# The indexer's projections cut into column blocks of 256 and 328 instead of 512 and 72

## The chip, the cores and the metric

The kernel runs on one core of one Trainium2 chip. The metric is the device time of one execution in microseconds (us). The core's engines are named as the profile names them: PE multiplies matrices (PEld is its weight load), DVE is the vector engine, ACT the activation engine, POOL the general one, SP issues DMAs. Work is ordered between engines by semaphores that the program sets by hand.

## The reference

One transformer block with a sparse attention, a gated unit and experts is followed by two more layers of another kind. The change touches the beginning of the first block alone, the projections of the attention's indexer, with 256 tokens of width 1024:

```python
proj = xn @ w_in[l]
q, k, v, qi, ki, wi, su, sv, ga, gb = split_columns(proj)
qi = rope(qi.reshape(B, L, IDX_HEADS, IDX_DIM), positions)   # 8 heads of 64
ki = rope(ki[:, :, None, :], positions)[:, :, 0]             # one head of 64
...
rel = jax.nn.relu(jnp.einsum('bqhd,bsd->bqhs', qib, ki))
score = jnp.einsum('bqh,bqhs->bqs', wb, rel).astype(jnp.float32)
_, sel = lax.top_k(score, top_k)
```

`qi` has 512 columns, `ki` 64 and `wi` (the gate of each indexer head) 8; they stand side by side in `w_in`. The score of each earlier token chooses the 64 keys that the attention sees.

## The kernel before

**Blocks and units.** `weight_block` cuts the weights into column blocks of up to 512 columns (L127), in the order in which they are used: q0, q1, qi, kw, k0, k1, v0, v1 and so on. A block of 1024 rows is one piece of the ring: SP loads it into one of two raw slots. It is then split into four units of two row chunks each. For each unit ACT rounds the raw numbers to the matmul's input type (`w_high`, L1517), POOL subtracts to get the rest (`w_low`, L852), and PE multiplies: per row chunk k and token tile t three matmuls, high times high (L925), high times w_low (L926) and x_low times w_high (L927). A block of eight chunks is 48 matmuls, whatever its width; the width is the number of columns that each streams. PE starts a unit when its `w_low` is made; POOL goes through the units in order; SP loads piece n when all `w_low` of piece n - 2 are made (`raw_free`). The product of a block lies in one of two pairs of PSUM banks, by the parity of the block's number, and the next block of the same parity waits until it has been moved out (`lin_moved`).

**What stands between the blocks.** DVE first works out the rotation angles (L2068 to L2082), in which each of the two token tiles begins with a multiplication of the frequencies by the position, from SBUF to SBUF (L2072). ACT takes sine and cosine of them (L1612, L1613), then copies q1 out of PSUM (L1539), then makes the w_high of kw (L1517), then takes its share of the transposes of the gated unit's weights `sgu_w` (L1615). Those are four jobs of two 128x128 transposes each on PE (L973), called by `sgu_weights` within qi at its chunks 4 and 5, two jobs at each; DVE copies the first and the third out of PSUM (L2091) and ACT the second and the fourth. There are two PSUM buffers for such jobs, so the third waits until DVE has taken the first, the fourth until ACT has taken the second. POOL masks the transposed weights after the fourth (L859), and its queue has this mask between the w_low of qi and those of kw.

**The rotation.** When qi is done DVE rotates its eight heads with `rotate_block` (L2101, L2102, L2104: two multiplications and one sum for each half of a head and each token tile, 12 instructions), then frees the bank, which k0 waits for. When kw is done DVE makes `wi` (L2112) and rotates the one key head, writing it twice side by side into `ki_twice`. k0 transposes both at its chunk 6, after later constants: `turn("qi", 4, ...)` and `turn("ki", 1, ...)`. After k1, PE forms the scores of the eight indexer heads (L1094).

Of the kernel before, what the change touches and what calls it, by code (L numbers as in the profile page):

```python
# [25 lines left out]
ALU = mybir.AluOpType  # L26
# [3 lines left out]
P = 128  # L30
SEQ = 256
TILES = SEQ // P
# [88 lines left out]
def program(nc, io, upto=99, tap=None):  # L121
# [3 lines left out]
    def weight_block(name, sources, width):  # L125


        rows = sources[0][0].shape[0]
        used = []
        for k0 in range(0, rows // P, 8):  # L130
            kn = min(8, rows // P - k0)
            loads, at = [], 0
            for w, c0, n in sources:
                loads.append((kn, width, at, n, w[k0 * P:(k0 + kn) * P, c0:c0 + n].rearrange("(k p) n -> p k n", p=P)))
                at += n
            used.append((len(pieces), k0, kn))
            pieces.append(loads)
        blocks[name] = (len(blocks), used, width)
# [2 lines left out]
    starts = dict(q=0, k=1024, v=2048, qi=3072, kw=3584, su=3656, sv=4680, ga=5704, gb=6728)  # L141
    for name in ("q", "k", "v", "su", "sv", "ga", "gb"):
        if name == "k":
            weight_block("qi", [(w_in, starts["qi"], 512)], 512)
            weight_block("kw", [(w_in, starts["kw"], 72)], 72)
        for j in range(2):
            weight_block(f"{name}{j}", [(w_in, starts[name] + j * NB, NB)], NB)

# [88 lines left out]
    with ctx:  # L237
# [70 lines left out]
        def buf(i, words=2048, at=0):  # L308
            return work[:, 2048 * i + at:2048 * i + at + words]

        def tok(view, t=TILES):
            return view.rearrange("p (t n) -> p t n", t=t)
# [131 lines left out]
        scaled_x = tok(buf(5))  # L444
        merged = tok(buf(4))
        v_tok, su, sv, ga, gb = (tok(buf(i)) for i in (5, 6, 7, 8, 9))
        qi_roped = tok(buf(9, 1024, 1024))
        qi_T = feat(buf(8, 1024))
        ki_twice = tok(buf(8, 256, 1168))
        ki_T = buf(8, 512, 1424).rearrange("p (e s) -> p e s", e=2)  # L450
        y_attn = tok(buf(2))
        relu2 = attn[:, 0:1024].rearrange("p (b t s) -> p b t s", b=2, t=TILES)
# [150 lines left out]
        def lin_out(name):  # L603
            o, _, width = blocks[name]
            return lin_ps[:, 2 * (o % 2):2 * (o % 2) + 2, 0:width]
# [297 lines left out]
        def _(pe):  # L903
            def linear(name, high, low, ready=None, rows_apart=0):


                o, used, width = blocks[name]
                if o >= 2:
                    pe.wait_ge(lin_moved[o % 2], o // 2)
                out = lin_out(name)  # L910
                last_k = used[-1][1] + used[-1][2] - 1
                block_units = [(k0 + UNIT_K * i, unit) for n, k0, _ in used for i, unit in enumerate(unit_views(n))]

                def products(first_k, unit, rows, prepare):
                    u, slot, words, _ = unit
                    if prepare:
                        pe.wait_ge(low_made, u + 1)
                    wh, wl = (w[:, slot, 0:words].rearrange("p (k n) -> p k n", n=width) for w in (w_high, w_low))
                    for j in range(words // width):
                        k = first_k + j  # L920
                        if ready and prepare:
                            ready(k)
                        for t in rows:
                            at = slice(P * t, P * (t + 1))
                            pe.matmul(out[:, t, :], high(k)[:, at], wh[:, j, :], start=(k == 0), stop=False)  # L925
                            pe.matmul(out[:, t, :], high(k)[:, at], wl[:, j, :], start=False, stop=False)  # L926
                            mm = pe.matmul(out[:, t, :], low(k)[:, at], wh[:, j, :], start=False, stop=(k == last_k))  # L927
                    return mm

                together = len(block_units) - rows_apart  # L930
                for first_k, unit in block_units[:together]:
                    products(first_k, unit, range(TILES), True).then_inc(units_used, 1)
                if rows_apart:
                    for first_k, unit in block_units[together:]:
                        mm = products(first_k, unit, (0,), True)
                    mm.then_inc(first_rows, 1)
                    for first_k, unit in block_units[together:]:
                        products(first_k, unit, (1,), False).then_inc(units_used, 1)
# [26 lines left out]
            def turn(name, n, src, first=0):  # L965

                for i in range(first, n):
                    k = jobs[name] + i
                    if k >= 2:
                        pe.wait_ge(tr_moved[k % 2], k // 2)  # L970
                    for c0, view in src(i):
                        rows_in_view = view.shape[0]
                        mm = pe.transpose(tr_ps[0:view.shape[1], k % 2, c0:c0 + rows_in_view], view,  # L973
                                          ident[0:rows_in_view, 0:rows_in_view])
                    mm.then_inc(tr_done, 1)
# [10 lines left out]
            def made(name):  # L986
                return lambda k: parts_made(pe, name, k + 1)

            def both(x):

                return lambda i: [(P * t, x[:, t, P * i:P * (i + 1)]) for t in range(TILES)]

            def small_out(pe, name):

# [58 lines left out]
            def amid(at, *what):  # L1053

                def ready(k):
                    if k == at:
                        for do in what:
                            do()
                return ready
# [22 lines left out]
            def later_columns():  # L1082
                pe.wait_ge(later_rows_in, 16 * (len(row_loads()) - 1))
                turn("later_cols", 1, lambda i: [(0, rows[0:104, 0, :]), (104, rows[0:120, 1, :]), (224, rows[0:88, 2, :])])

            linear("k0", *from_x, ready=amid(6, later_columns, lambda: pe.wait_ge(roped, 2), lambda: turn("qi", 4, both(qi_roped)),
                                             lambda: turn("ki", 1, both(ki_twice))))
            linear("k1", *from_x)
            tr_wait(pe, "ki", 1)
            for i in range(IDX_HEADS):  # L1090
# [878 lines left out]
        def _(dve):  # L1969
            order = [0]  # L1970

            def step(ins):

                order[0] += 1
                ins.then_inc(dve_order, 1)
                dve.wait_ge(dve_order, order[0])
# [116 lines left out]
            def rotate_block(dst, src, heads, cos, sin):  # L2093

                m = sc_ps[:, 0, 0:32 * heads].rearrange("p (h j) -> p h j", h=heads)
                for t in range(TILES):
                    x = src[:, t, :].rearrange("p (h a j) -> p h a j", h=heads, a=2)
                    c, s = (cs[:, t, :].unsqueeze(1).broadcast_to([P, heads, 32]) for cs in (cos, sin))
                    for a, op in ((0, ALU.subtract), (1, ALU.add)):
# [3 lines left out]
                        for y in (*others, first):  # L2103
                            step(dve.tensor_tensor(y, first, m, op))  # L2104

            lin_ready(dve, "qi")
            rotate_block(lambda t: [qi_roped[:, t, :].rearrange("p (h a j) -> p h a j", h=IDX_HEADS, a=2)], lin_out("qi"),
                         IDX_HEADS, cos1[:, :, 64:96], sin1[:, :, 64:96])
            dve.sem_inc(lin_moved[blocks["qi"][0] % 2], 1)
            dve.sem_inc(roped, 1)  # L2110
            lin_ready(dve, "kw")
            step(dve.tensor_tensor(wi[:], lin_out("kw")[:, :, 64:72], rest.unsqueeze(2).broadcast_to([P, TILES, IDX_HEADS]), ALU.mult))  # L2112
            rotate_block(lambda t: [ki_twice[:, t, 64 * c:64 * c + 64].rearrange("p (h a j) -> p h a j", h=1, a=2)
                                    for c in range(2)], lin_out("kw")[:, :, 0:64], 1, cos1[:, :, 64:96], sin1[:, :, 64:96])
            dve.sem_inc(lin_moved[blocks["kw"][0] % 2], 1)
            dve.sem_inc(roped, 1)
            step(dve.memset(ki_T, 0.0))
            dve.wait_ge(tr_done, jobs["later_cols"] + 1)
            dve.tensor_copy(cols[:, KC:312], tr_ps[:, jobs["later_cols"] % 2, KC:312]).then_inc(tr_moved[jobs["later_cols"] % 2], 1)
# [527 lines left out]
```

## Time and profile before

| | us |
| --- | --- |
| median of 3 runs | 1339.53 |
| lowest and highest run | 1337.6 and 1340.6 |
| span of the profiled execution | 1341.4 |
| PE busy in it | 1252.6 (93%) |
| POOL busy | 770.9 (57%) |
| ACT busy | 639.0 (48%) |
| DVE busy | 461.8 (34%) |

The span runs from the first to the last instruction of one profiled execution; it lies 1.9 us above the median of the timed runs and 0.8 us above the slowest of them. PE is the busiest engine by far, but its busy time counts a matmul from its start to its modelled end, so that matmuls overlap in it: how fast PE goes is read from the distance between the starts of two. The granted clock of PE (PEclk) is a share of 2.4 GHz; the profile shows two levels, 1.00 and 0.50 (1.2 GHz).

### The profile page before, as it was taken

The numbers are of one execution on the slowest core, as the hardware profiler recorded it, in microseconds if no ns is written. First come the engines' busy times: TensorE is split into PE (matmuls) and PEld (weight loads), VectorE is DVE, ScalarE is ACT, GpSimd is POOL, SyncE is SP. The second block draws the span as 40 slices with busy tenths as digits, with TensorE's granted clock in tenths as the row PEclk, the third lists the DMA queues.
The fourth block names the chain that finished last, engine by engine and source line by source line (L and its number), as shares of the span: only waits on it lengthen the run. The fifth ranks groups of instructions, "written<-read, shape, count | busy, mean of one in ns | idle before, by whom it ended". The sixth has DMA issues, their size and how long they took to land.

```text
span 1341.4 us, 19669 instructions
## 1 busy us (share of the span) xinstructions
PE 1252.6 (93%) x7904; PEld 1029.7 (77%) x7904; DVE 461.8 (34%) x1047; ACT 639.0 (48%) x1108; POOL 770.9 (57%) x345
## 2 busy tenths in 40 slices
PE   8999999998887887999899999999999889999998
PEld 6888877776342333887789999888997778999986
DVE  3527333433121112355613332102468272322311
ACT  6445544643111011745636655436797444655552
POOL 5868985440000000982048988888689805788884
PEclk8999999998998999998999999999999999999999
DMA  6635554396999999553034655644535503455552
GB/s 241 218 128 189 188 189 158 110 367 262 423 421 420 414 422 412 184 182 111 1 106 147 227 183 178 219 162 153 183 129 186 187 19 124 142 179 185 189 188 79
DMA packets 126449, 275.09 MB, mean 205 GB/s; under 512 B 7524, under 2 KB 53916, under 8 KB 114076
## 3 DMA queue, kind: packets, MB, share of 16 engines
q1 hardware_dynamic: 126076, 272.86, 55.8%
q8 instruction: 58, 0.95, 0.3%
q10 hardware_dynamic: 288, 1.05, 0.2%
q14 instruction: 27, 0.22, 0.0%
HBM read 272.85 MB, written 1.05 MB: 204 GB/s over the span
## 4 chain that ended last, share of the span: by engine, by line
PE 75%; ACT 7%; DMA 7%; DVE 5%; POOL 4%; issue 2%; POOLq 0%; SPq 0%; DVEq 0%; ACTq 0%
PE lin_ps L925 11%; PE lin_ps L927 11%; PE lin_ps L926 11%; PE lin_ps L955 8%; PE lin_ps L958 8%; PE lin_ps L957 8%; DMA ring<-in_w_expert_in 5%; PE sc_ps L1218 4%; POOL w_low L852 4%; ACT w_high L1517 2%; PE lin_ps L1235 2%; PE lin_ps L1041 2%; PE sc_ps L1010 2%; PE lin_ps L1203 1%; PE tr_ps L1020 1%
## 5 line engine op out<-in xcount | busy, mean ns | idle before, releaser
L852 POOL TENSOR_TENSOR w_low<-ring,w_high 128x1024 fp32r<-128x1024 f32 (+1 forms) x318 | 762.1, 2432 | 551.5 <-ACT w_high L1517 551.3
L1517 ACT ACTIVATE w_high<-ring 128x1024 fp32r<-128x1024 f32 (+1 forms) x320 | 312.8, 1043 | 139.0 <-PE lin_ps L927 78.7
L955 PE MATMUL lin_ps<-x_high,w_high 128*128 128x256 f32 x960 | 272.8, 284 | 0.0
L957 PE MATMUL lin_ps<-x_high,w_low 128*128 128x256 f32 x960 | 271.6, 283 | 0.0
L958 PE MATMUL lin_ps<-x_low,w_high 128*128 128x256 f32 x736 | 208.3, 283 | 0.0
L957 PEld LDWEIGHTS lin_ps<-x_high,w_low 128*128 128x128 f32 x960 | 184.2, 192 | 0.1
L955 PEld LDWEIGHTS lin_ps<-x_high,w_high 128*128 128x128 f32 x960 | 184.2, 192 | 0.1
L925 PE MATMUL lin_ps<-w_high,x_high 128*128 128x512 f32 (+1 forms) x432 | 170.5, 395 | 5.6 <-POOL w_low L852 2.7
L926 PE MATMUL lin_ps<-w_low,x_high 128*128 128x512 f32 (+1 forms) x432 | 168.1, 389 | 0.0
L927 PE MATMUL lin_ps<-w_high,x_low 128*128 128x512 f32 (+1 forms) x368 | 143.1, 389 | 0.0
L958 PEld LDWEIGHTS lin_ps<-x_low,w_high 128*128 128x128 f32 x736 | 141.2, 192 | 0.0
L925 PEld LDWEIGHTS lin_ps<-w_high,x_high 128*128 128x128 f32 x432 | 82.0, 190 | 22.9 <-DVE w_low L2059 2.8
L926 PEld LDWEIGHTS lin_ps<-w_low,x_high 128*128 128x128 f32 x432 | 82.2, 190 | 15.9
L927 PEld LDWEIGHTS lin_ps<-w_high,x_low 128*128 128x128 f32 x368 | 70.1, 191 | 14.4
L1218 PE MATMUL sc_ps<-ring,work 128*32 128x512 f32 x496 | 62.6, 642 | 14.6 <-DMA ring<-in_w_expert_in 10.2
L1798 ACT ACTIVATE attn<-lin_ps,cols 128x256 f32<-128x256 f32 x44 | 18.5, 472 | 114.7 <-PE lin_ps L958 114.7
L925 PE MATMUL lin_ps<-w_high,hidden_high 128*128 128x512 f32 x176 | 68.7, 390 | 0.7 <-POOL w_low L852 0.7
L926 PE MATMUL lin_ps<-w_low,hidden_high 128*128 128x512 f32 x176 | 68.5, 389 | 0.0
L927 PE MATMUL lin_ps<-w_high,hidden_low 128*128 128x512 f32 x176 | 68.5, 389 | 0.0
L2413 DVE SCALAR_TENSOR_TENSOR attn<-lin_ps,cols,attn 128x255 f32<-128x255 f32 x44 | 21.1, 479 | 124.9 <-ACT attn L1798 124.9
L958 PE MATMUL lin_ps<-u_low,w_high 128*128 128x256 f32 x224 | 63.4, 283 | 0.0
L1218 PEld LDWEIGHTS sc_ps<-ring,work 128*32 128x32 f32 x496 | 16.5, 117 | 53.2 <-issue 38.8
(430 smaller groups left out, 1921.7 us busy)
## 6 DMA issues: line engine op xcount, KB each, us to landing
ring<-in_w_expert_in SPq DMA_DIRECT2D x31, 2048.0 KB, 14.3
ring<-in_ffn_w_in SPq DMA_DIRECT2D x44, 1024.0 KB, 7.7
ring<-in_w_in SPq DMA_DIRECT2D x13, 2048.0 KB, 7.8
ring<-in_b_w_in SPq DMA_DIRECT2D x11, 2048.0 KB, 8.0
work<-in_w_expert_out SPq DMA_DIRECT2D x8, 2048.0 KB, 23.0
ring<-in_w_expert_out SPq DMA_DIRECT2D x8, 2048.0 KB, 17.6
ring<-in_ffn_w_out SPq DMA_DIRECT2D x8, 2048.0 KB, 8.0
ring<-in_a_w_in SPq DMA_DIRECT2D x4, 2048.0 KB, 8.2
```

The lines of the kernel that those rows point to most:

```text
L852: pool.tensor_tensor(w_low[:, slot, 0:words], raw, w_high[:, slot, 0:words].bitcast(F32), ALU.subtract).then_inc(low_made, 1)
L925: pe.matmul(out[:, t, :], high(k)[:, at], wh[:, j, :], start=(k == 0), stop=False)
L926: pe.matmul(out[:, t, :], high(k)[:, at], wl[:, j, :], start=False, stop=False)
L927: mm = pe.matmul(out[:, t, :], low(k)[:, at], wh[:, j, :], start=False, stop=(k == last_k))
L955: pe.matmul(out, wh[:, j, at], high(k), start=(k == 0 and f < 2), stop=False, skip_group_check=True)
L957: pe.matmul(out, wl[:, j, at], high(k), start=False, stop=False, skip_group_check=True)
L958: mm = pe.matmul(out, wh[:, j, at], low(k), start=False, stop=(k == last_k), skip_group_check=True)
L1010: mm = pe.matmul(sc_ps[:, g % 2, SEQ * t:SEQ * t + n], q(i, t), k(i)[:, 0:n], start=True, stop=True)
L1041: mm = pe.matmul(out[:, dim * t:dim * (t + 1)], pT[:, P * n:P * (n + 1)], v(i, c), start=(c == 0), stop=(c == chunks[-1][0]))
L1218: mm = pe.matmul(hid_ps[CAP * e:CAP * (e + 1), :], gathered[:, 4 * a + k, CAP * e:CAP * (e + 1)], extra_slot(e)[:, k, :] if extra and a == ...
L1235: mm = pe.matmul(y_ps[CAP * e:CAP * (e + 1), n, :], act_T[:, P * f + CAP * e:P * f + CAP * (e + 1)], w, start=(f == 0), stop=(f == 1))
L1517: act.activation(w_high[:, slot, 0:words], raw, ACT.Copy).then_inc(high_made, 1)
```

## The change

The same 584 columns are projected in two blocks of another cut. qi now has the first 256 columns (four query heads); kw has the other 328 (four query heads, the key, the gate). Both are still 48 matmuls and four units. `rotate_block` runs on four heads after qi, and on five (four query heads and the key) after kw, and one more DVE copy doubles the rotated key. The rotated heads of kw lie in a new view `qk_roped`, which replaces `ki_twice`; the transposes read from both views, as many as before.

```diff
-            weight_block("qi", [(w_in, starts["qi"], 512)], 512)
-            weight_block("kw", [(w_in, starts["kw"], 72)], 72)
+            weight_block("qi", [(w_in, starts["qi"], 256)], 256)
+            weight_block("kw", [(w_in, starts["qi"] + 256, 328)], 328)
...
-        qi_roped = tok(buf(9, 1024, 1024))
+        qi_roped = tok(buf(9, 512, 1024))
+        qk_roped = tok(buf(6, 768, 1024))
         qi_T = feat(buf(8, 1024))
-        ki_twice = tok(buf(8, 256, 1168))
...
-            linear("k0", *from_x, ready=amid(6, later_columns, lambda: pe.wait_ge(roped, 2), lambda: turn("qi", 4, both(qi_roped)),
-                                             lambda: turn("ki", 1, both(ki_twice))))
+            linear("k0", *from_x, ready=amid(6, later_columns, lambda: pe.wait_ge(roped, 2), lambda: turn("qi", 2, both(qi_roped)),
+                                             lambda: turn("qi", 4, both(qk_roped, 2), first=2),
+                                             lambda: turn("ki", 1, both(qk_roped, -2))))
...
             lin_ready(dve, "kw")
-            step(dve.tensor_tensor(wi[:], lin_out("kw")[:, :, 64:72], rest.unsqueeze(2).broadcast_to([P, TILES, IDX_HEADS]), ALU.mult))
...
+            step(dve.tensor_tensor(wi[:], lin_out("kw")[:, :, 320:328], rest.unsqueeze(2).broadcast_to([P, TILES, IDX_HEADS]), ALU.mult))
+            rotate_block(lambda t: [qk_roped[:, t, 0:320].rearrange("p (h a j) -> p h a j", h=5, a=2)],
+                         lin_out("kw")[:, :, 0:320], 5, cos1[:, :, 64:96], sin1[:, :, 64:96])
             dve.sem_inc(lin_moved[blocks["kw"][0] % 2], 1)
-            dve.sem_inc(roped, 1)
+            dve.tensor_copy(qk_roped[:, :, 320:384], qk_roped[:, :, 256:320]).then_inc(roped, 1)
             step(dve.memset(ki_T, 0.0))
```

The order of the queues stays; the sizes in them change. On POOL, from the first constants to the block v1 (`w_low` is the rest of a unit's weights, `xqT` holds the gated unit's transposed weights):

```order
 L840 MEMSET eps 128x1
-L852 TENSOR_TENSOR w_low<-ring,w_high 128x1024 x10
+L852 TENSOR_TENSOR w_low<-ring,w_high 128x1024 x6
+L852 TENSOR_TENSOR w_low<-ring,w_high 128x512 x4
 L859 AFFINE_SELECT xqT<-xqT 128x1024
-L852 TENSOR_TENSOR w_low<-ring,w_high 128x144 x4
+L852 TENSOR_TENSOR w_low<-ring,w_high 128x656 x4
 L852 TENSOR_TENSOR w_low<-ring,w_high 128x1024 x16
```

The four units of qi halve and the four of kw grow from 144 to 656 columns; the mask still stands between them.

On ACT, from the sine to the first units behind kw, before:

```order
L1612 ACTIVATE attn<-sc_ps 128x192
L1613 ACTIVATE attn<-sc_ps 128x192
L1539 ACTIVATE work<-lin_ps,small 128x512 x2
L1517 ACTIVATE w_high<-ring 128x144 x4
L1615 ACTIVATE xqT<-tr_ps 128x256 x2
```

and after (every line number of ACT is one higher):

```order
L1613 ACTIVATE attn<-sc_ps 128x192
L1614 ACTIVATE attn<-sc_ps 128x192
L1540 ACTIVATE work<-lin_ps,small 128x512 x2
L1518 ACTIVATE w_high<-ring 128x656 x4
L1616 ACTIVATE xqT<-tr_ps 128x256 x2
```

The two copies of transposed weights (`xqT`) stay behind the w_high of kw, which are 656 columns wide now.

## Rows read from the trace of the kernel before

**Rows 1.** The page's part 4: the chain that ended last, by engine.

```profile
PE 75%; ACT 7%; DMA 7%; DVE 5%; POOL 4%; issue 2%; POOLq 0%; SPq 0%; DVEq 0%; ACTq 0%
```

**Rows 2.** Timeline of PE, qi to k0: start us, us, engine, line, instruction, [idle before].

```profile
37.32 0.39 PE L925 MATMUL lin_ps<-w_high,x_high 128*128 128x512 f32 x1
...
42.76 0.60 PE L973 MATMUL tr_ps<-ident,work 128*128 128x128 f32 x4
...
44.59 0.60 PE L973 MATMUL tr_ps<-ident,work 128*128 128x128 f32 x4
...
49.27 0.28 PE L927 MATMUL lin_ps<-w_high,x_low 128*128 128x72 f32 x1
...
54.30 0.28 PE L927 MATMUL lin_ps<-w_high,x_low 128*128 128x72 f32 x1
54.95 0.72 PE L925 MATMUL lin_ps<-w_high,x_high 128*128 128x512 f32 x1 [0.36 <-DVEq L2109]
...
58.70 0.39 PE L925 MATMUL lin_ps<-w_high,x_high 128*128 128x512 f32 x1
...
64.83 0.66 PE L973 MATMUL tr_ps<-ident,work 104*128 104x104 f32 x5
...
70.11 0.39 PE L925 MATMUL lin_ps<-w_high,x_high 128*128 128x512 f32 x1
```

**Rows 3.** Stretch of k0: length; busy PE, PEld, DVE, ACT, POOL; PEclk; DMA share; GB/s.

```profile
54.95:58.46 3.51, 3.51 (x9) 2.73 (x10) 2.83 (x15) 0.43 (x1) 3.51 (x3) 0.51 0.26 96
```

**Rows 4.** Timeline of PE in the second feed-forward: matmuls of 256 columns.

```profile
759.77 0.28 PE L955 MATMUL lin_ps<-x_high,w_high 128*128 128x256 f32 x1
...
761.93 0.28 PE L955 MATMUL lin_ps<-x_high,w_high 128*128 128x256 f32 x1
```

**Rows 5.** Timeline of DVE: the end of the angles, their scaling, the two rotations.

```profile
34.85 2.25 DVE L2072 TENSOR_SCALAR work<-work,pos_f 128x96 f32<-128x96 f32 x1
...
40.11 0.27 DVE L2082 TENSOR_SCALAR sc_ps<-sc_ps 128x96 f32<-128x96 f32 x1
41.00 1.60 DVE L2090 TENSOR_SCALAR attn<-attn,small 128x32 f32<-128x32 f32 x4 [0.62 <-ACT attn L1613]
...
49.34 0.42 DVE L2101 TENSOR_TENSOR work<-lin_ps,attn 128x256 f32<-128x256 f32 x1 [3.90 <-PE lin_ps L927]
...
56.26 0.19 DVE L2101 TENSOR_TENSOR work<-lin_ps,attn 128x32 f32<-128x32 f32 x1
```

**Rows 6.** Timeline of POOL: units of qi, the mask, units of kw, of k0 and k1.

```profile
32.26 9.47 POOL L852 TENSOR_TENSOR w_low<-ring,w_high 128x1024 fp32r<-128x1024 f32 x4 [0.79 <-ACT w_high L1517]
45.68 1.09 POOL L859 TENSOR_SCALAR_AFFINE_SELECT xqT<-xqT 128x1024 f32<-128x1024 f32 x1 [3.95 <-ACT xqT L1615]
46.75 1.86 POOL L852 TENSOR_TENSOR w_low<-ring,w_high 128x144 fp32r<-128x144 f32 x4
50.90 18.78 POOL L852 TENSOR_TENSOR w_low<-ring,w_high 128x1024 fp32r<-128x1024 f32 x8 [2.28 <-ACT w_high L1517]
```

**Rows 7.** Timeline of ACT: units of qi, the sine, q1, units of kw, k0, k1.

```profile
31.12 3.91 ACT L1517 ACTIVATE w_high<-ring 128x1024 fp32r<-128x1024 f32 x4 [1.00 <-DMA ring<-in_w_in]
...
40.41 0.33 ACT L1612 ACTIVATE attn<-sc_ps 128x192 f32<-128x192 f32 x1 [4.08 <-DVE sc_ps L2082]
...
40.85 1.27 ACT L1539 ACTIVATE work<-lin_ps,small 128x512 f32<-128x512 f32 x2
41.99 0.98 ACT L1517 ACTIVATE w_high<-ring 128x144 fp32r<-128x144 f32 x4
...
49.76 3.91 ACT L1517 ACTIVATE w_high<-ring 128x1024 fp32r<-128x1024 f32 x4 [4.15 <-DMA ring<-in_w_in]
58.03 3.91 ACT L1517 ACTIVATE w_high<-ring 128x1024 fp32r<-128x1024 f32 x4 [4.36 <-DMA ring<-in_w_in]
```

**Rows 8.** Timeline of PE late in the program: a wait, after which the clock is low.

```profile
1103.03 0.66 PE L1428 MATMUL tr_ps<-ident,work 128*128 128x128 f32 x2 [2.09 <-DVE o_low L2603]
```

**Rows 9.** Stretch after that wait, columns as in rows 3.

```profile
1103.00:1106.00 3.00, 2.97 (x8) 2.47 (x9) 0.76 (x2) 0.48 (x1) 0.00 (x0) 0.50 0.00 0
```

More of the change, by code:

```diff
@@ L987, in made, with both @@
                 return lambda k: parts_made(pe, name, k + 1)
-            def both(x):
-                return lambda i: [(P * t, x[:, t, P * i:P * (i + 1)]) for t in range(TILES)]
+            def both(x, before=0):
+                return lambda i: [(P * t, x[:, t, P * (i - before):P * (i - before + 1)]) for t in range(TILES)]
             def small_out(pe, name):
@@ L2106, in _ @@
             lin_ready(dve, "qi")
-            rotate_block(lambda t: [qi_roped[:, t, :].rearrange("p (h a j) -> p h a j", h=IDX_HEADS, a=2)], lin_out("qi"),
-                         IDX_HEADS, cos1[:, :, 64:96], sin1[:, :, 64:96])
+            rotate_block(lambda t: [qi_roped[:, t, :].rearrange("p (h a j) -> p h a j", h=4, a=2)], lin_out("qi"),
+                         4, cos1[:, :, 64:96], sin1[:, :, 64:96])
             dve.sem_inc(lin_moved[blocks["qi"][0] % 2], 1)
@@ L2111, in _ @@
             lin_ready(dve, "kw")
-            step(dve.tensor_tensor(wi[:], lin_out("kw")[:, :, 64:72], rest.unsqueeze(2).broadcast_to([P, TILES, IDX_HEADS]), ALU.mult))
-            rotate_block(lambda t: [ki_twice[:, t, 64 * c:64 * c + 64].rearrange("p (h a j) -> p h a j", h=1, a=2)
-                                    for c in range(2)], lin_out("kw")[:, :, 0:64], 1, cos1[:, :, 64:96], sin1[:, :, 64:96])
+            step(dve.tensor_tensor(wi[:], lin_out("kw")[:, :, 320:328], rest.unsqueeze(2).broadcast_to([P, TILES, IDX_HEADS]), ALU.mult))
+            rotate_block(lambda t: [qk_roped[:, t, 0:320].rearrange("p (h a j) -> p h a j", h=5, a=2)],
+                         lin_out("kw")[:, :, 0:320], 5, cos1[:, :, 64:96], sin1[:, :, 64:96])
             dve.sem_inc(lin_moved[blocks["kw"][0] % 2], 1)
-            dve.sem_inc(roped, 1)
+            dve.tensor_copy(qk_roped[:, :, 320:384], qk_roped[:, :, 256:320]).then_inc(roped, 1)
             step(dve.memset(ki_T, 0.0))
```

## The prediction

> **What bounds the kernel now.** I read the chain of work that ended last first: three quarters of it is PE [rows 1]. So a change in the first block's projections is worth what it takes from PE's timeline there, and after it from whatever PE waits for. Then I read PE's timeline from the start of qi to the start of k1 [rows 2]. qi begins at 37.32 and has done 24 of its 48 matmuls at 42.76: 5.44 / 24 = 0.227 us each. kw goes in steps of (54.30 - 49.27) / 45 = 0.112 us, though it streams a seventh of the columns. Then k0 waits 0.36 us for DVE and starts at 54.95, and its first nine matmuls take until 58.70, 0.417 us each. The granted clock says why: in that stretch it is 0.51, the lower of the two levels [rows 3], and what PE did before was kw's 48 narrow matmuls and the short wait. k1 starts at 70.11. Last come the queues that feed the stretch: DVE's angles and rotations [rows 5], POOL's units [rows 6], ACT's [rows 7].
>
> **PE's own work.** A matmul of 256 columns goes at (761.93 - 759.77) / 18 = 0.120 us [rows 4]. No row shows 328 columns. Bounds are 0.120 and 0.227; on the line between them it is 0.120 + 72 / 256 x 0.107 = 0.150, which I take, since the nearer row is 256 (by the lower bound kw would be 1.4 us shorter, by the upper 3.7 longer). qi: 48 x (0.227 - 0.120) = 5.1 saved. kw: 48 x (0.150 - 0.112) = 1.8 paid. Taken alone that is 3.3 us less.
>
> The Trainium skill, TensorE: Matmul & The Clock Gate, section "Back-to-back issue gap", gives N / 2.4 + 2.5 ns for a gap. By it, 256 columns are 109 ns and 328 are 139; the trace's 120 for 256 differs and decides, and by the page's figure kw would be 48 x 11 ns = 0.5 us shorter and the time 1337.5, an estimate from that page.
>
> **A wait takes most of it.** The transposes of sgu_w stand inside qi, at its chunks 4 and 5, and they need other engines that do not come sooner because PE does. PE would reach the first pair at 37.32 + 24 x 0.120 = 40.2 instead of 42.76. It can do jobs 1 and 2, six matmuls and job 3; job 4 needs ACT to have copied job 2, and ACT's queue has sine, cosine, the copy of q1 and the w_high of kw ahead of that copy, the last now 656 columns wide instead of 144. So the end hangs on DVE's angles, which start ACT's sine.
>
> DVE: the second multiplication of L2072 began at 34.85 and took 2.25 us, eight times the 0.27 of a neighbour of the same width [rows 5]. It ended at 37.10, while POOL's second unit of qi ended at 32.26 + 2 x 2.37 = 37.00 [rows 6]: it was held until that unit was over. With 512 columns a unit takes, on the line from 0.465 (144) to 2.37 (1024), 1.26 us. POOL was free from 31.47 (0.79 before 32.26), and ACT, which waited 1.00 for the weights until 31.12 [rows 7], is ready at 30.12 when half the bytes are to land. So the units end at 32.7, 34.0, 35.26 and 36.5, and DVE is let go at 35.36, 1.74 us sooner. The angles end at 38.64 instead of 40.38. The Trainium skill, SBUF — State Buffer, section "SBUF: two separate sides", calls the ports that DVE and GpSimd share an exclusive lock, held for a whole instruction. By that rule the gain is these 1.74 us and the second rival below is out; the trace's 0.10 between the two ends agrees, and that it is one pair of ends keeps the rival in.
>
> ACT: all is 1.74 sooner up to kw, so q1 is copied from 39.11 and the units of kw start at 40.25. One takes, between 0.245 and 0.98 [rows 7], 0.67; four end at 42.94, just as before (41.99 + 0.98). Copying job 2 takes some 0.4: 43.3. PE has by then stood since about 41.4, 1.9 us.
>
> POOL: from the start of the second pair of jobs to the mask it was 45.68 - 44.59 = 1.09; with one job only left, some 0.85. The mask starts at 44.2, the units of kw 1.07 later at 45.3, each 1.57 long (the same line): the first is made at 46.84, the last at 51.6. PE ends qi at 43.3 + 0.3 + 18 x 0.120 = 45.8, waits 1.1 for the first unit, and does kw in 48 x 0.150 = 7.2, until 54.1; POOL's later units are ahead of it. k0 starts at 54.2 instead of 54.95: **0.75 us** sooner. Of 3.3 + 0.5 us, about 3 went into the two waits.
>
> **The clock.** If kw at 328 columns keeps PE at the full level, the nine matmuls of k0 take 9 x 0.227 instead of 3.75: **1.7 us** less. Bounds: 0 (it falls all the same, or the timed runs of before don't pay it) to 1.7. From there to k1 nothing changes in length: 36 matmuls and the 5.28 us from 64.83 to 70.11 [rows 2]. k1 starts at 54.2 + 8.2 + 5.3 = 67.7 instead of 70.1.
>
> **What is late next.** DVE rotates four heads after qi: at 128 columns, between 0.19 and 0.42 [rows 5], about 0.33 a step with its wait, 12 steps, 4.0 us from 46.0: done at 50, so k0 waits for nothing there, where it did before. After kw come wi, 12 steps of 160 columns (0.36), 4.5 us: 58.8. The new copy of the key is SBUF to SBUF, as L2072 is, so it can be held by a unit of POOL for up to 2.37: 61.2. PE asks for it at chunk 6 of k0, 54.2 + 8.2 = 62.4. It costs nothing with 1.2 us in hand, and up to 1 us if kw ends late against POOL. The weights: k0 is loaded once qi's w_low are made, which is sooner; ACT found k0 landed at 49.76 and POOL is not free for it before 51.6. k1 is loaded once kw's w_low are made, 51.6 instead of 48.61 (46.75 + 1.86), so it lands about 3 us later than 58.03 at most, and ACT ends its units at 65 at most, where it should copy the first transposes of k0 at 63: between 0 and 0.7 us on PE through the fourth of those jobs; I take 0.1. Load issues, semaphores and the memory layout I cost at nothing: as many DMAs of as many rows, and SP still has the same small loads ahead of k0.
>
> **Sum.** On the profiled execution 0.75 + 1.7 - 0.1 = 2.35 us, 1341.4 to 1339.05. What follows is fed by PE's own progress, so I carry it whole. The median of before lies 1.9 below this span, and whether the timed runs pay the low clock at k0 no row shows. I count half of it: 0.75 + 0.85 - 0.1 = 1.5, and 1339.5 - 1.5 = **1338.0**.
>
> **The rivals.**
> 1. *It does what it says:* PE is 3.3 shorter in its matmuls, the 0.5 before k0 and the 1.7 of clock go, no wait comes instead: 5.5 us, 1334.0. This needs job 4 and POOL's first unit of kw in time for a PE that is 2.6 us ahead. Against it: ACT's queue. 8%.
> 2. *Slower:* the angles don't come sooner, because DVE is not let in between two of POOL's short units. The units of kw on ACT then end at 44.7, job 2 is copied at 45.1, the first w_low of kw comes at 48.5, and PE stands 3.6 us. After a wait of 2.09 the clock was low elsewhere [rows 8, 9], so the rest of qi at about 0.21 us a matmul ends at 49.2 and part of kw is slow: k0 starts near 57, 2 us late, less the half of the clock that it had lost: 1340.7. It decides at a release of DVE after about 36.2. For it: nothing but a lock that I read from two ends; against it, the same rows. 15%.
> 3. *The clock falls in the new 1.9 us wait* (the nearest rows: [rows 8, 9]): the rest of qi takes 3.8 instead of 2.2, of which 1.1 is hidden by the wait for kw, and some of kw may be slow, together 0.5 to 1.3: 1338.9. 17%.
>
> The other 5% is for what no row here shows.
>
> **How the numbers follow.** The forecast has 55%. The three runs of before spread 1.9 below and 1.1 above the median, and the clock term is 0.85 either way: the forecast reaches from 1336 to 1340. With rival 2 and its spread above, and a third of what rival 1 adds below, 8 in 10 lie in 1335.5 to 1341.2. A measurement can tell 0.2%, 2.7 us, from no change. Faster by that: rival 1 and the lowest quarter of the forecast, 22%. Slower: the upper end of rival 2, 6%. Within: 72%.
>
> **What would show it.** After the change: L2072's second instruction at 0.5 us instead of 2.25; PE idle about 1.9 before a transpose in qi, put down to ACT's copy, and about 1.1 before kw's first matmul, put down to POOL; 328 columns at 0.150; k0 without a wait and at clock 1.00; k1 near 67.7. The forecast is wrong if the waits in qi and kw together are under 1 us or over 4.5, or if k0 is slow all the same.

## The result and the profile after

| | before | after |
| --- | --- | --- |
| median, us | 1340.70 (22 runs) | 1343.47 (22 runs) |
| lowest to highest, us | 1337.6 to 1343.6 | 1338.71 to 1346.44 |
| span of the profiled execution, us | 1341.4 | 1342.3 |

The ratio after to before is 1.0018, with a 95% interval of 1.0010 to 1.0025: the changed kernel is slower, by a fifth of a per cent. 1338.0 was forecast, in a range up to 1341.2. The line numbers of PE, POOL and SP are those of before, those of ACT and DVE one higher; in an experiment they move by the lines that its edit adds.

**PE** first, the timeline that answers to [rows 2] (start us, us, engine, line, instruction, [idle before <- who ended it]):

```profile
36.78 0.28 PE L925 MATMUL lin_ps<-w_high,x_high 128*128 128x256 f32 x1
...
42.66 0.44 PE L973 MATMUL tr_ps<-ident,work 128*128 128x128 f32 x2 [1.47 <-ACT xqT L1616]
...
46.38 0.39 PE L925 MATMUL lin_ps<-w_high,x_high 128*128 128x328 f32 x1 [1.14 <-POOL w_low L852]
46.61 0.31 PE L926 MATMUL lin_ps<-w_low,x_high 128*128 128x328 f32 x1
...
53.50 0.31 PE L927 MATMUL lin_ps<-w_high,x_low 128*128 128x328 f32 x1
57.52 0.77 PE L925 MATMUL lin_ps<-w_high,x_high 128*128 128x512 f32 x1 [3.71 <-POOL w_low L852]
...
68.63 0.66 PE L973 MATMUL tr_ps<-ident,work 104*128 104x104 f32 x5
```

Up to the end of kw it goes as forecast. From qi's start to kw's last matmul are 53.50 - 36.78 = 16.72 us, with one wait in qi and one before kw; before it was 54.30 - 37.32 = 16.98. Then PE stands 3.71 us before k0, where it stood 0.36 [rows 2]. From qi's start to k0's transposes are 68.63 - 36.78 = 31.85 us against 64.83 - 37.32 = 27.51: 4.3 us are lost in this stretch.

The wait is put down to POOL. POOL's timeline answers to [rows 6] (the last unit of q1 and the four of qi, the four of kw, the first three of k0):

```profile
28.53 7.42 POOL L852 TENSOR_TENSOR w_low<-ring,w_high 128x1024 fp32r<-128x1024 f32 x5
...
44.66 6.27 POOL L852 TENSOR_TENSOR w_low<-ring,w_high 128x656 fp32r<-128x656 f32 x4
55.02 7.03 POOL L852 TENSOR_TENSOR w_low<-ring,w_high 128x1024 fp32r<-128x1024 f32 x3 [4.09 <-ACT w_high L1518]
```

POOL waited 4.09 us for ACT. ACT's timeline answers to [rows 7]:

```profile
39.65 2.69 ACT L1518 ACTIVATE w_high<-ring 128x656 fp32r<-128x656 f32 x4
...
53.89 3.90 ACT L1518 ACTIVATE w_high<-ring 128x1024 fp32r<-128x1024 f32 x4 [10.37 <-PE lin_ps L927]
```

ACT stood 10.37 us before k0's units. The name behind that wait is PE, whose kw block ended at about the same time; what ACT also waited for is k0's weights, as the timeline of the DMA queue of SP tells. First of before (kw's load, the first long ones of the small loads, k0's load):

```profile
31.50 0.37 SPq L665 DMA_DIRECT2D ring<-in_w_in  x1
...
32.54 0.87 SPq L676 DMA_DIRECT2D router_w<-in_w_router_expert  x1
33.45 0.86 SPq L701 DMA_DIRECT2D work<-in_norm_g  x1
...
40.89 0.47 SPq L710 DMA_DIRECT2D cs<-in_rope_sin  x1
41.76 0.37 SPq L665 DMA_DIRECT2D ring<-in_w_in  x1
```

The same of after:

```profile
30.97 0.37 SPq L665 DMA_DIRECT2D ring<-in_w_in  x1
...
32.01 1.54 SPq L676 DMA_DIRECT2D router_w<-in_w_router_expert  x1
33.59 2.85 SPq L701 DMA_DIRECT2D work<-in_norm_g  x1
...
43.03 0.47 SPq L710 DMA_DIRECT2D cs<-in_rope_sin  x1
43.54 0.47 SPq L665 DMA_DIRECT2D ring<-in_w_in  x1
```

The issues of kw's and of k0's weights of after by the view of DMA issues (KB, us from issue to landing); in before they were 288 KB in 3.6 us and 2048 KB in 7.9:

```profile
ring<-in_w_in SPq DMA_DIRECT2D x1, 1312.0 KB, 6.2
...
ring<-in_w_in SPq DMA_DIRECT2D x1, 2048.0 KB, 10.2
```

Between the two loads SP issues the same nineteen small ones. Two of them take (1.54 - 0.87) + (2.85 - 0.86) = 2.66 us longer, now that the load ahead of them has 1312 KB instead of 288. In before SP was done with them at 41.36, just before the slot of k0's load came free with qi's last w_low (32.26 + 9.47 = 41.73 [rows 6]). In after that slot is free at 28.53 + 7.42 = 35.95, by POOL's row of qi's units, and SP comes at 43.54: what k0's load waits for is no longer POOL but SP. The load then takes 10.2 us instead of 7.9. It lands at 53.8, when PE has finished kw; ACT's and POOL's first units add the rest of the 3.71 us. So of the 4.1 us by which it lands later, 1.8 are the later issue and 2.3 the load itself.

Where the 2.3 us are, the landings in the trace tell. A load counts as landed when the last of its sixteen parts is in. In after fifteen parts of k0's load were in at 52.12 and the last at 53.78; in before these were 49.63 and 49.65. So 1.6 us are one late part. The DMA queue that the profile names "instruction" moved one packet of 16 KB in that time, from 51.41 and for 1.06 us. This goes together in all sixteen traces: of the 113 loads into the ring that land between 15 and 100 us, 21 have a last part 0.8 us or more behind the fifteenth, and in each of the 21 such a packet had begun while the load was under way. That the packet is what holds the part up is argued from this and not shown. In before the packet fell into k1's load (from 53.82), for which PE did not wait. For the rest of the 2.3 us the trace has only that at 44 to 46 us the DMA engines are still busy with the small loads (share 0.67 at 95 GB/s).

The clock is low behind the wait: it fell within it, between 56 and 57 us. The stretch of k0 that answers to [rows 3] (length; busy PE, PEld, DVE, ACT, POOL; PEclk; DMA share; GB/s):

```profile
57.50:63.60 6.10, 6.08 (x14) 4.84 (x15) 2.56 (x5) 4.18 (x5) 6.10 (x3) 0.50 0.09 35
63.60:68.60 5.00, 5.00 (x23) 4.08 (x22) 0.00 (x0) 0.00 (x0) 5.00 (x3) 1.00 0.62 200
```

Fourteen matmuls of k0 run at the low level, nine before. From k0's start to its transposes are 11.11 us instead of 9.88. So the 4.3 us are: 3.4 more wait before k0, 1.2 more low clock in it, and 0.3 saved up to kw's end.

The spans differ by 0.9 only. A part of the rest is in stretches that have nothing to do with the change: over the whole span the mean granted clock was 0.984 in the profile of before and 0.992 in that of after. At 311 us, for one, it was low in before and not in after (columns as above). Of before:

```profile
311.10:317.80 6.70, 6.70 (x33) 6.70 (x33) 4.31 (x27) 5.22 (x5) 0.00 (x0) 0.50 1.01 429
```

and of after:

```profile
311.10:317.80 6.70, 5.25 (x43) 4.75 (x42) 4.51 (x16) 5.34 (x9) 0.00 (x0) 1.00 0.78 293
```

Why it falls there in one execution and not in another these runs don't say. The medians differ by 2.8; how the 4.3 us of the one trace become that over 22 runs no trace shows.

### The profile page after: what moved, and what is told of

Read it like the earlier page. It is cut to its first block, busy times and chain, and to the rows that moved or that the text cites. A ratio compares the mean times of both kernels' runs of the same rounds, so it can differ in the third digit from the quotient of the medians.

```text
span 1342.3 us, 19665 instructions
## 1 busy us (share of the span) xinstructions
PE 1244.6 (93%) x7904; PEld 1023.1 (76%) x7904; DVE 459.8 (34%) x1044; ACT 637.4 (47%) x1108; POOL 770.7 (57%) x345
## 4 chain that ended last, share of the span: by engine, by line
PE 70%; DMA 9%; ACT 8%; DVE 5%; POOL 4%; issue 2%; SPq 0%; POOLq 0%; DVEq 0%; ACTq 0%
PE lin_ps L925 10%; PE lin_ps L927 10%; PE lin_ps L926 10%; PE lin_ps L955 8%; PE lin_ps L958 8%; PE lin_ps L957 8%; DMA ring<-in_w_expert_in 5%; POOL w_low L852 4%; PE sc_ps L1219 3%; ACT w_high L1518 3%; DMA work<-in_w_expert_out 2%; PE lin_ps L1041 2%; PE sc_ps L1010 2%; PE lin_ps L1236 1%; PE lin_ps L1204 1%
## 5 line engine op out<-in xcount | busy, mean ns | idle before, releaser
L925 PE MATMUL lin_ps<-w_high,x_high 128*128 128x512 f32 (+2 forms) x432 | 169.8, 393 | 10.0 <-POOL w_low L852 7.5
L926 PE MATMUL lin_ps<-w_low,x_high 128*128 128x512 f32 (+2 forms) x432 | 167.0, 387 | 0.0
L927 PE MATMUL lin_ps<-w_high,x_low 128*128 128x512 f32 (+2 forms) x368 | 141.9, 386 | 0.0
```

## The experiments

My theory after the result: kw's wider load holds SP's small loads up, k0's load goes out and lands late, and both the wait at k0 and the low clock in it come from that. The rival: the two waits in qi and before kw (1.47 and 1.14 us) push the rest back and lower the clock. Each ratio is to the kernel before on the same chip, and its median stands beside it.

**1 and 2. k0's load ahead of the small loads**, in the changed kernel and in the one before:

```diff
-                if n == RAW + 2:
+                if n == RAW + 3:
                     load_router()
```

> The changed kernel with one move on SP: the small loads (router, constants, gains) are issued behind k0's weights instead of ahead of them. Theory: in the changed kernel k0's weights landed at 53.78 us because kw's larger load (1312 KB instead of 288) stalled SP in the small loads, and k0's load came behind them. Then k0 now lands before 46, PE starts k0 within 0.5 us of kw's end and at the full clock, k1 starts 5 to 6.5 us sooner than in the changed kernel (73.9), and the time falls by 4 to 6 us, to 1337.5 to 1339.5. Rival one (the two new waits of PE, 1.47 us in qi and 1.14 before kw, make the loss): the time stays within 1 us of 1343.5. Rival two (the low clock in k0 comes from kw's matmuls and not from the wait): k0 starts sooner but still slow, and the time falls by 2 to 3 us only.

Measured: 1339.78 (before 1340.42), ratio 1.0005, 0.9987 to 1.0023, just above the 1337.5 to 1339.5 that I expected; one of the 12 runs took 1350.42. The load goes out at 36.90 and takes 8.2 us; no wait is left before k0. From qi's start to k0's transposes are 64.26 - 37.88 = 26.38 us instead of 31.85. The longest wait of PE's timeline from qi to k1 is now:

```profile
44.84 0.44 PE L973 MATMUL tr_ps<-ident,work 128*128 128x128 f32 x2 [1.92 <-ACT xqT L1616]
```

and the stretches behind it, with the columns of [rows 3], are:

```profile
45.60:49.00 3.40, 3.40 (x18) 3.33 (x17) 0.19 (x1) 0.30 (x2) 3.22 (x3) 0.50 0.16 43
49.00:64.00 15.00, 15.00 (x83) 13.61 (x83) 10.52 (x26) 6.65 (x8) 15.00 (x8) 1.00 0.58 186
```

The clock is low only behind the wait in qi (from 45.6), and full in k0. In the timed runs the gain is less plain than in the trace: by the medians 3.4 us of the changed kernel's loss are gone ((1343.47 - 1340.70) - (1339.78 - 1340.42)), by the ratios (1.0018 and 1.0005) 1.7, and the intervals of the ratios overlap.

> The kernel before with the same move on SP. Theory: k0's load waits there until the last unit of qi is made by POOL (41.73), when the small loads are already issued, so the move gives nothing: k0 lands within 0.5 us of 49.65, and the time is within 1.5 us of the kernel before. If the move is worth something by itself, whatever the cut of the blocks, the time falls by 2 us or more here too.

Measured: 1345.96, ratio 1.0044, 1.0029 to 1.0058: slower, against what I expected. The small loads now stand between k0's load and k1's, and behind a load of 2048 KB they hold SP even longer (3.12 and 3.11 us). k1's load goes out at 53.73, and ACT makes its units when it should copy k0's transposes. ACT's timeline:

```profile
62.72 3.90 ACT L1517 ACTIVATE w_high<-ring 128x1024 fp32r<-128x1024 f32 x4 [11.91 <-DMA ring<-in_w_in]
```

and PE's:

```profile
66.93 0.66 PE L973 MATMUL tr_ps<-ident,work 128*128 128x128 f32 x4 [2.23 <-ACT work L1555]
```

So the move helps only where k0's load is what is late, and passes the delay on to the next load.

**3. The kernel before with a larger load of kw.** A further load of 1024 KB goes out behind kw's, into a part of the raw slot that nothing reads; columns, units and matmuls stay at 512 and 72.

```diff
+                if n == 3:
+                    sp.dma_start(ring[:, 1, 2048:4096]..., w_in[:, 3072:3328]...).then_inc(weights_in[1], 16)
```

> The kernel before, whose kw load is followed by one more load of 256 columns (1 MB) into a part of the ring that nothing reads, counted with kw's: the bytes of the changed kernel without its matmuls, units and waits. Theory: SP stalls in the small loads as in the changed kernel (about 2.5 us), k0's weights land at 52 to 54 instead of 49.65, PE starts k0 at 56 to 57.6 instead of 54.95, and the time is 1 to 3 us over the kernel before. Rival (the waits of PE in qi and kw, or the units' sizes, make the loss): within 1 us of the kernel before.

Measured: 1345.87, ratio 1.0043, 1.0027 to 1.0058, more than the 1 to 3 us that I expected. The kernel before gets the changed kernel's loss, and more, as it has not the saving in qi. SP's queue:

```profile
33.49 1.79 SPq L679 DMA_DIRECT2D router_w<-in_w_router_expert  x1
35.32 2.66 SPq L704 DMA_DIRECT2D work<-in_norm_g  x1
...
45.07 0.47 SPq L665 DMA_DIRECT2D ring<-in_w_in  x1
```

and PE's first matmul of k0, whose load took 10.3 us here (its last part at 55.41, the fifteenth at 53.89):

```profile
59.14 0.77 PE L928 MATMUL lin_ps<-w_high,x_high 128*128 128x512 f32 x1 [4.48 <-POOL w_low L855]
```

So more bytes ahead of SP's small loads, without the changed columns and their waits, are enough to make the wait before k0. Here they came with a second load of as many rows; that the bytes count and not the rows is seen where one load of 1024 rows stands there in each case (last section).

**4. The wait in qi taken away.** ACT copies the transposed weights before it makes kw's units, in the changed kernel:

```diff
-            copy_scaled("q1", half(q_raw, 1))
+            copy_scaled("q1", half(q_raw, 1), then_split=False)
             tr_take(act, 0, "sgu_w", 4, ...)
+            split_to(piece("q1") + 2)
```

> The changed kernel with one move on ACT: its two copies of the transposed sgu weights come ahead of its units of kw instead of behind them. PE's wait in qi should go (1.47 us) and most of that before kw (1.14), so kw ends 1.5 to 2.5 us sooner. Theory: k0 still starts when its weights have landed (about 53.8 plus 3.7), so the time stays within 1.5 us of the changed kernel (1343.5). Rival (those two waits make the loss): 1340.5 to 1341.5.

Measured: 1344.24, ratio 1.0026, 1.0014 to 1.0038, no better than the changed kernel. The wait in qi is gone, and what it held back arrives earlier at the same late load. The wait before kw, which I expected to shrink too, stays. PE's timeline:

```profile
44.80 0.39 PE L925 MATMUL lin_ps<-w_high,x_high 128*128 128x328 f32 x1 [1.14 <-POOL w_low L852]
57.41 0.77 PE L925 MATMUL lin_ps<-w_high,x_high 128*128 128x512 f32 x1 [5.18 <-POOL w_low L852]
```

1.47 us less in qi, 1.47 us more before k0. The rival falls: as long as k0's load is late, what PE reaches sooner only waits longer for it. Behind this longer wait the clock is low up to 60.8 only, where in the changed kernel it was up to 63.6: the length of the wait does not settle how long the clock stays low.

**5. Both.** The edits of 1 and 4 together.

> The changed kernel with both edits: k0's load issued ahead of the small loads, and ScalarE copying q1 for TensorE before it splits kw's weights. Theory: alone the second edit gave nothing, because the wait that it removes in qi (1.47 us) came back at k0, which waited for its load. With k0's load early, nothing is late there, so the wait in qi and the low clock that follows it (45.6 to 49.0, 3.4 us at half speed, about 1.7 us) both go: 1.5 to 3 us under the run with k0's load first alone, so 1337 to 1338.5 where the kernel before takes 1340.5. Rival: the wait only moves to kw's first matmul (kw's weights are split 1.3 us later, POOL makes its first rest later), the clock falls all the same: 1339.5 to 1341.

Measured: 1340.38 (before 1340.74), ratio 0.9996, 0.9984 to 1.0008, not the 1337 to 1338.5 expected. The wait in qi is gone and the clock is full until PE stands at k0's transposes, so the rival is not the reason. As in 2, k1's load is now the late one (issued 51.87, its units on ACT from 60.25), and PE stands for ACT at k0's transposes:

```profile
64.47 1.85 PE L973 MATMUL tr_ps<-ident,work 128*128 128x128 f32 x6 [2.64 <-ACT work L1556]
```

**6 and 7. The small loads before kw's load**, where SP waits some 9 us for a slot anyway: in the changed kernel and in the kernel before.

```diff
-                if n == RAW + 2:
+                if n == RAW + 1:
```

> The changed kernel with the small loads (router, rows, gains, tables) put one piece sooner, between qi's and kw's weights, in a stretch where SyncE waits 9.4 us for the ring slot of kw's weights. Theory: k0's load is issued as soon as its slot is free (about 36.9, landing about 45), and k1's load keeps its time too (51 to 59), so k0 starts without a wait: 1338 to 1340, like the run with k0's load first or a little under. Rival: the small loads stall on SyncE behind qi's 1024 KB as they did behind kw's 1312 KB, kw's load is issued 2 us or more later than 30.97, ScalarE waits for it at 39.65 and TensorE at kw: 1341 to 1344.

Measured: 1340.83, ratio 1.0023, 1.0004 to 1.0042, above the 1338 to 1340 expected: eight of twelve runs lie between 1337.9 and 1341.8, four between 1345.9 and 1350.1. In the profiled run, one of the eight, kw's load goes out at 33.48, 2.5 us later, and ACT is ready for it 0.4 us before it lands. k0 and k1 come without a wait for a load. PE waits 1.93 us in qi, as in 1. What the four had no profile shows.

> The kernel before with the same move of the small loads as in the run above. Theory: the loss of 5 us in the kernel before with k0's load first came from k1's load alone, which the small loads then held back (issued 53.7, landed 62.6). Here both k0's and k1's loads are early, so that loss is gone: 1339.5 to 1341.5, no gain either, since the kernel before waits only 0.36 us at k0, and not for its load. Rival: an early load of k0 hurts by itself (it shares the DMA engines with other loads, or ScalarE splits k0's weights ahead of what TensorE waits for): 1344 to 1346 as there.

Measured: 1340.42, ratio 0.9998, 0.9989 to 1.0008. The loss of 2 is gone, so it was k1's late load, and the kernel before has nothing to gain here: its k0 waited for no load.

**8 to 10. Small loads before kw and ACT's copies first**: the changed kernel with the edits of 4 and 6, the kernel before with the same, and the first once more beside it.

> The changed kernel with the small loads between qi's and kw's weights and ScalarE copying q1 before it splits kw's weights. Theory: no wait of over 1.2 us is left from qi to k1, the clock stays at full speed from there, 1336 to 1338.5. Rival: kw's weights, split later and loaded later, make TensorE wait 2.5 us or more at kw's first matmul, and the clock falls: 1340 to 1343.

> The kernel before (512 and 72 columns) with both moves: the small loads between qi's and kw's weights, and ScalarE copying q1 before it splits kw's weights. Theory: TensorE of the kernel before waits neither for a load nor for ScalarE's copies in qi, kw and k0, so neither move has anything to take away: 1339.5 to 1341.5, the same as the kernel before (1340.7). Then what the changed kernel gains with the same two moves is the worth of its columns. Rival: the two moves gain by themselves, whatever the columns: 1336 to 1338.

> The changed kernel (256 and 328 columns) with the same two moves, beside the run above on one chip. Theory: it saves the 3.3 us of matmuls that the narrower columns save on paper (5.1 less in qi, 1.8 more in kw), loses some 1.2 of it to one wait before kw's first matmul, and its first 512-column block meets the low clock no more (1.7): 1336.5 to 1338, with the interval of the ratio below 1. Rival: its 1337.0 was luck in where the clock fell later in the program: 1339.5 to 1341.

Measured: the changed kernel 1336.99, ratio 0.9979 (0.9959 to 1.0000), and again 1342.65, ratio 1.0011 (0.9984 to 1.0038); the kernel before 1339.92, ratio 0.9998 (0.9985 to 1.0012). The two moves give the kernel before nothing. In the profiled run of the first, qi to k0's transposes takes 61.93 - 37.90 = 24.03 us, 3.5 less than before, with one wait of 1.16 us, and the clock is full throughout. PE's timeline, and the stretch of kw and k0:

```profile
37.90 0.28 PE L925 MATMUL lin_ps<-w_high,x_high 128*128 128x256 f32 x1
...
61.93 0.66 PE L973 MATMUL tr_ps<-ident,work 104*128 104x104 f32 x5
```

```profile
46.00:62.00 16.00, 15.54 (x85) 14.08 (x86) 9.45 (x25) 7.00 (x9) 16.00 (x9) 1.00 0.42 137
```

But the 24 runs fall into two groups, 16 from 1332 to 1340.5 and 8 from 1345 to 1349.6, and the mix of the two decides the median. The first median came as expected and the second did not, with 2 and 6 of its 12 runs in the upper group.

**11 and 12. That kernel again**, unchanged, for a profile of the upper group.

> The changed kernel with both moves, looked at once more, since its 24 runs fall into two groups (16 from 1332 to 1340.5, 8 from 1345 to 1349.6). Theory: in the slow group the clock falls between qi and k1, after the 1.15 us wait before kw, as it fell after the waits of the changed kernel: a low stretch of 3.4 or 6.8 us begins there and k0's transposes start 2 us or more after 62. Rival: the stage from qi to k1 is as short as in the fast group (its transposes end 25.8 to 26.5 us after qi's start), and what is lost is lost later in the program.

> The same kernel, for a profile of the slow group if the run above is of the fast one; expected as there.

Measured: 1344.12 and 1336.7, one run each; the first lies just under the upper group and far over the lower. Neither theory had it. In the first, a copy of 128x128 numbers on DVE, the doubling of the rotated key, takes 11.24 us, and PE stands 7.49 us for it. The timelines of DVE, POOL and PE there:

```profile
54.32 11.24 DVE L2118 COPY work<-work 128x128 f32<-128x128 f32 x1
```

```profile
51.47 14.01 POOL L852 TENSOR_TENSOR w_low<-ring,w_high 128x1024 fp32r<-128x1024 f32 x6
```

```profile
65.62 0.69 PE L973 MATMUL tr_ps<-ident,work 128*128 128x128 f32 x2 [7.49 <-DVE work L2118]
```

In the second the same copy takes 1.91 (DVE, POOL):

```profile
56.92 1.91 DVE L2118 COPY work<-work 128x128 f32<-128x128 f32 x1
```

```profile
53.97 9.47 POOL L852 TENSOR_TENSOR w_low<-ring,w_high 128x1024 fp32r<-128x1024 f32 x4
```

POOL's units run one behind the other, some 2.35 us each. In the second run the copy ends at 58.83, with POOL's second unit (53.97 + 2 x 2.37 = 58.71). In the first it began in POOL's second unit, was not let in at the end of that one or of the three after it, and ended at 65.56, when POOL had nothing more to do (51.47 + 14.01 = 65.48): PE stood, so no slot came free for another unit.

**13 and 14. The key doubled by ACT**, which waits for k1's weights at that time: in the kernel of 8, and alone in the changed kernel.

```diff
-            dve.tensor_copy(qk_roped[:, :, 320:384], qk_roped[:, :, 256:320]).then_inc(roped, 1)
+            dve.sem_inc(key_roped, 1)
...
                 lin_ready(act, name)
+                if name == "kw":
+                    act.wait_ge(key_roped, 1)
+                    act.activation(qk_roped[:, :, 320:384], qk_roped[:, :, 256:320], ACT.Copy).then_inc(roped, 1)
                 split_to(piece(name) + 2)
```

> The changed kernel with both moves, and the doubling of the rotated key done by ScalarE instead of VectorE (ScalarE stands idle there, waiting for k1's weights until about 57). Theory: the slow third of the runs is VectorE's copy of the key alone, which takes 1.9 us where it gets in between two of GpSimd's units and 11.2 us where it does not, and TensorE then stands 7.5 us at k0's transposes. ScalarE's copy takes some 0.3 us whatever GpSimd does, so the slow group is gone: median 1335 to 1337.5, hardly a run above 1341, ratio to the kernel before below 0.999. Rival: the 11.2 us are a sign of something else that strikes there (a stall of all engines, or the opening without a low clock), and hits the next instruction instead: again a third of the runs at 1345 to 1349.6.

Measured: 1337.02 (1331.82 to 1339.1, before 1341.18), ratio 0.9968, 0.9954 to 0.9982. No run of the upper group is left, and this version is 0.3% faster than the kernel before. Beside the changed kernel with only the copy moved (experiment 14, on the same chip) it is 6.4 us faster by the medians. ACT's copy, and PE's qi and first transposes of k0:

```profile
56.63 0.31 ACT L1623 ACTIVATE work<-work 128x128 f32<-128x128 f32 x1 [7.57 <-DVEq L2122]
```

```profile
36.44 0.28 PE L926 MATMUL lin_ps<-w_high,x_high 128*128 128x256 f32 x1
...
59.89 0.66 PE L974 MATMUL tr_ps<-ident,work 104*128 104x104 f32 x5
```

> The changed kernel with only the key's doubling moved to ScalarE. Theory: there k0 starts 3.7 us late for its load, and VectorE's copy (58.5) has ten us until TensorE asks for it at 68.6, so being held costs little: 1342 to 1344, no better than the changed kernel (1343.5). Rival: a good part of the changed kernel's loss was this copy, in runs that the profile did not show: 1340 to 1341, and fewer runs above 1344.

Measured: 1343.46, ratio 1.0018, 1.0004 to 1.0032, the same as the changed kernel. There the copy (1.30 us, from 58.49) is ready long before 68.6, so it has no part in the loss that the change showed.

## Why the prediction was wrong

**PE's own work: right.** 256 columns go at (39.53 - 36.78) / 23 = 0.120 us, up to the transposes in qi, and 328 at (53.50 - 46.61) / 46 = 0.150. The formula of the Trainium skill's page TensorE: Matmul & The Clock Gate, section "Back-to-back issue gap", that stands beside my sum is given there for a matmul by itself, not for a stream with weight loads as here; it came out 11 ns low for both widths (109 and 139).

**The release of DVE: right.** L2072's second instruction, L2073 now, takes 0.43 us instead of 2.25 [rows 5], and ACT's sine starts at 38.07 instead of 40.41:

```profile
34.33 0.43 DVE L2073 TENSOR_SCALAR work<-work,pos_f 128x96 f32<-128x96 f32 x1
```

It ended at 34.76, right behind POOL's third unit of qi (by 1.26 us a unit at 35.95 - 1.26 = 34.69). This agrees with the lock of the section "SBUF: two separate sides" of SBUF — State Buffer in the Trainium skill. The earlier sine rules out the second rival.

**The two waits: right in kind, a little over in size.** 1.47 was measured where 1.9 was forecast in qi, and 1.14 where 1.1 was before kw; ACT's four units took 2.69 as worked out. The clock stayed full through both here. That the third rival was not idle the first experiment shows: behind a wait of 1.92 in qi the clock was low for 3.4 us.

**The weights and the load issues: the step that failed.** "k0 is loaded once qi's w_low are made, which is sooner" and "Load issues ... I cost at nothing: as many DMAs of as many rows, and SP still has the same small loads ahead of k0." Qi's last w_low is indeed made 5.8 us sooner, but SP comes to k0's load only at 43.54, since it works through the small loads first, and two of them take longer behind a larger load. I counted the DMAs that SP issues and did not look at how long SP is busy with them. The rows were there in before: its queue ended the small loads 0.4 us before k0's slot came free, so nothing of an earlier slot could be had, and right behind kw's load two of them took 0.87 and 0.86 us where others take 0.28 to 0.65. The load landed 4.1 us later than at 49.65, 1.8 of it by the issue and 2.3 by the load, which I had taken to be as quick as before. POOL took up k0 at 55.02, where the cover that I named was "not free for it before 51.6": 3.4 us short. In the sum this is the term of k0 without a wait. From qi's start to k0's transposes I had 62.4 - 37.32 = 25.1 us and it took 31.85; 3.7 of the difference are the wait before k0, 2.9 the clock behind it (11.11 against 8.2).

**The clock at k0: right as a mechanism, hidden by the failed step.** It was forecast full and was low for fourteen matmuls, but behind a wait of 3.71 us. Where that wait is taken away and kw keeps its 328 columns (experiments 1, 8 and 13) k0 runs at full clock; with kw at 72 columns and no wait before k0 but 0.35 us it begins at the low clock again (experiment 9: its first matmul takes 0.72, as in [rows 2]). I counted half of this clock in the median; the profiled executions give no reason for the half, as k0 was at the low clock in all five with 72 columns (before and experiments 2, 3, 7 and 9).

**The copy of the key: held longer than I allowed.** I bounded it by one unit of POOL, 2.37 us, and it can be five, 11.24 us. In the changed kernel itself that cost nothing; in the kernel of experiments 8 and 10 the upper 8 runs of 24 have a mean 10 us over that of the others (1346.4 and 1336.2). One run with the long copy was profiled; that the others had it too is concluded from experiment 13, where with the copy on ACT none of 12 runs is like them.

**The sum.** With the late load, the wait in qi and the held copy out of the way, the changed columns bring 1341.18 - 1337.02 = 4.2 us (the first two moves alone give the kernel before nothing, experiment 9), between the 1.5 forecast and the 5.5 of the first rival; in the stretch from qi to k0's transposes it is 27.51 - (59.89 - 36.44) = 4.06.

## What to carry to other kernels

When a change makes one load larger, read the issuing engine's own timeline behind it: loads queued there, and every later load behind those, move with the bytes ahead of them, though their number stays. A wait that ends on a split or a copy is followed back to the load's issue, and only then costed. And an SBUF to SBUF instruction on DVE beside a row of POOL instructions should be bounded by the whole row, not by one of them, or given to ACT. A load is in when its last part is in, so its time from issue to landing is not a constant to carry over.

## What the runs showed of the hardware

SP stalls at the same two small loads of its queue, by the size of the load issued just ahead of them: 0.87 and 0.86 us behind 288 KB, 1.21 and 2.53 behind 1024 KB (experiment 8), 1.54 and 2.85 behind 1312 KB, 3.17 and 3.08 behind 2048 KB (experiment 1). Each of these is one load of 1024 rows. The loads behind them are issued in some 0.3 to 0.65 us each in all four.

The last of a load's sixteen parts landed 0.8 to 1.7 us behind the fifteenth in 21 of 113 loads, each time with a packet of 16 KB of the instruction queue begun while the load was under way; of the loads without one under way none had such a late part. The reverse does not hold: some loads had such a packet under way and no late part.

A DVE copy from SBUF to SBUF that meets a row of POOL units ended with the unit in which it began in seven profiled runs (0.44 to 1.98 us), with the next one in experiment 1 (4.12) and four units later in experiment 11 (11.24): at the end of a unit it is let in, or it is not, and what decides it no run here shows. ACT's copy of the same numbers beside the same row took 0.31 us.
